# Closing norm of an expert-choice encoder layer: where six tiles meet the norm's weight, and in which order the last rows go

## What is computed

```python
def expert_choice_sublayer(x, norm_g, w_router, w_gate, w_up, w_down):
    tokens = rms_norm(x, norm_g).reshape(n_tok, d)
    affinity = softmax(tokens @ w_router)
    gate, idx = lax.top_k(affinity.T, cap)      # cap = 128 of 1024 tokens, 32 of 256
    xe = tokens[idx]
    hid = silu(xe @ w_gate) * (xe @ w_up)
    ye = (hid @ w_down) * gate[..., None]
    out = zeros.at[idx.reshape(-1)].add(ye.reshape(-1, d))
    return x + out
y = rms_norm(x, final_g)   # y * rsqrt(mean(y*y) + eps) * final_g
```

## Time and profile before

| | us |
|---|---|
| median of 3 runs | 1298.23 (1298.19 to 1299.98) |
| the profiled execution | 1298.81 |
| its span, first to last instruction | 1297.1 |
| last TensorE product of the last expert ends | 1279.85 |
| last VectorE instruction ends | 1292.17 |
| last indirect DMA issued | 1293.37 |

### The profile page before, as it was taken

The page is one execution under the profiler, slowest core; times in us unless marked ns, Lnnn a source line. Parts: engine busy times, 40 slices in busy tenths (PEclk is TensorE's granted clock), DMA queues, the critical chain, the costliest instruction groups (busy, mean ns, idle before and its releaser), DMA issues.

```text
span 1297.1 us, 25116 instructions
## 1 busy us (share of the span) xinstructions
PE 1255.2 (97%) x9762; PEld 1032.7 (80%) x9814; DVE 905.8 (70%) x1298; ACT 742.0 (57%) x1079; POOL 323.1 (25%) x316
## 2 busy tenths in 40 slices
PE   8999999999999999779999999999999999999994
PEld 7868986666687888578888888898889888988892
DVE  6462122541586655978879888988898889888887
ACT  7645322222345544456677667766676667667764
POOL 2512221010133231141132313131313231223040
PEclk8999999999999999979999999999999999999998
DMA  8231544360278773288999999999999999999996
GB/s 274 66 122 50 163 146 137 108 180 25 75 248 248 226 213 116 90 302 290 329 300 315 327 332 294 321 333 319 299 315 340 313 306 318 332 310 309 295 351 271
DMA packets 242033, 314.76 MB, mean 243 GB/s; under 512 B 16097, under 2 KB 206049, under 8 KB 241969
## 3 DMA queue, kind: packets, MB, share of 16 engines
q1 hardware_dynamic: 226576, 268.54, 62.3%
q0 software_dynamic: 15392, 45.36, 12.0%
HBM read 274.41 MB, written 39.44 MB: 242 GB/s over the span
## 4 chain that ended last, share of the span: by engine, by line
PE 92%; DMA 2%; ACT 2%; DVE 2%; issue 1%; SPq 0%; POOL 0%; ACTq 0%; DVEq 0%; POOLq 0%
PE psum L2253 23%; PE psum L2114 15%; PE psum L2260 11%; PE psum L2081 9%; PE psum L1965 9%; PE psum L2276 9%; PE psum L2294 4%; PE psum L2285 4%; PE psum L2246 1%; PE psum L2027 1%; DMA eraw<-in_w_up_dram 1%; PE psum L2032 1%; ACT yt L1248 1%; PE psum L1987 1%; PE psum L1945 1%
## 5 line engine op out<-in xcount | busy, mean ns | idle before, releaser
L1812 DVE TENSOR_TENSOR elo<-eraw,ehi 128x2048 bf16<-128x2048 f32 x192 | 433.5, 2285 | 1.0 <-POOLq L822 1.0
L1218 ACT ACTIVATE ehi<-eraw 128x2048 fp32r<-128x2048 f32 x192 | 362.2, 1902 | 25.7 <-PE psum L2294 18.6
L2253 PE MATMUL psum<-xc,ehi 128*128 128x320 f32 x2048 | 332.3, 314 | 1.9 <-DVE xc L1817 1.9
L2253 PEld LDWEIGHTS psum<-xc,ehi 128*128 128x128 f32 x2048 | 304.2, 189 | 3.5 <-DVE xc L1817 2.3
L2260 PE MATMUL psum<-xb,elo 128*128 128x160 bf16 x2048 | 163.9, 233 | 0.0
L1825 DVE TENSOR_REDUCE gu<-psum 128x320 f32<-128x640 f32 x128 | 105.3, 823 | 82.0 <-PE psum L2260 81.8
L2260 PEld LDWEIGHTS psum<-xb,elo 128*128 128x128 bf16 x2048 | 138.5, 98 | 13.0
L2114 PE MATMUL psum<-hn_nar,wnar 128*128 128x512 bf16 (+1 forms) x748 | 141.2, 343 | 1.2
L2276 PE MATMUL psum<-ehi,hc 128*128 128x512 f32 x512 | 132.7, 406 | 0.0
L2114 PEld LDWEIGHTS psum<-hn_nar,wnar 128*128 128x128 bf16 x768 | 73.1, 98 | 63.0 <-issue 4.5
L2276 PEld LDWEIGHTS psum<-ehi,hc 128*128 128x128 f32 x512 | 95.2, 188 | 22.1
(11 more groups left out here) (290 smaller groups left out, 1664.2 us busy)
## 6 DMA issues: line engine op xcount, KB each, us to landing
eraw<-in_w_gate_dram SPq DMA_DIRECT2D x64, 1024.0 KB, 6.6
eraw<-in_w_up_dram SPq DMA_DIRECT2D x64, 1024.0 KB, 9.6
eraw<-in_w_down_dram SPq DMA_DIRECT2D x64, 1024.0 KB, 13.6
wraw<-in_w_in_dram SPq DMA_DIRECT2D x12, 1024.0 KB, 7.3
negm<-negm_d SPq DMA_DIRECT2D x10, 512.0 KB, 7.4
acc_d<-x POOLq DMA_DIRECT2D x10, 512.0 KB, 5.4
tok_d<-tk POOLq DMA_DIRECT2D x10, 512.0 KB, 2.9
v<-v_d SPq DMA_DIRECT2D x18, 256.0 KB, 4.3
```

What stands on the lines that cost most here:

```text
L1218: act.activation(f["ehi"][:, j % RING, :], f["eraw"][:, raw_slot(s, j), :], ACT.Copy).then_inc(S["ehi"], 1)
L1812: dve.tensor_tensor(f["elo"][:, j % RING, :], f["eraw"][:, raw_slot(s, j), :], f["ehi"][:, j % RING, :].bitcast(F32), ALU.subtract).then_i ...
L2253: pe.matmul(o[:, 0:2 * NC], hi[:, k, c], x[:, k, :, :].rearrange("p a t -> p (a t)"), start=(k == 0), stop=False, skip_group_check=True)
```

## The change

The weight's part of six scalings goes to GpSimd: for k = 4 to 9 it multiplies the tile by the norm's weight into a new tile `pre`, which lies over the first three `ehi` buffers. The first of these waits for the last gate and up product (`gu_ps`), the fifth for the last expert's first down step (`dn_ps`), each pair for its tiles to have landed. VectorE scales four of the products (k = 4, 5, 8, 9) by the root alone with a `tensor_scalar`, and ScalarE two (k = 6, 7) with an ACTIVATE Copy. The roots are made in three batches (4, 4, 2) instead of two (4, 6). The last expert's rows are taken before the roots of k = 8 and 9. ScalarE's squares of k = 4 to 9 leave their unused output in PSUM instead of `yt`. The last two scatters, and the scalings ahead of them, change places: samples first, prompt second.

```diff
@@ -316,7 +316,9 @@
         FINAL = [0, 1, 8, 9, 2, 3, 4, 5, 6, 7]
-        FINAL_BATCHES = [(0, 4), (4, NT)]
+        FINAL_BATCHES = [(0, 4), (4, 8), (8, NT)]
+        BY_ACT = (6, 7)
+        pre = overlay(size([("eraw", [P, RAW, PIECE], F32)]), ("pre", [P, 6, D], F32))["pre"]
 
@@ -637,7 +640,10 @@
             for k, n in enumerate(FINAL):
-                sp.wait_ge(S["f_y"], k + 1)
+                if k in BY_ACT:
+                    sp.wait_ge(S["f_y_act"], k - BY_ACT[0] + 1)
+                else:
+                    sp.wait_ge(S["f_y"], k + 1 if k < BY_ACT[0] else k - 1)
                 sp.dma_start(y_chunk[n], final_tile(n)).then_inc(S["f_out_p" if n < NTP else "f_out"], 16)
@@ -861,17 +867,25 @@
             i.then_inc(S["f_same"], 1)
+            pool.wait_ge(S["gf_in"], 16 * 5)
+            for k in range(4, NT):
+                pool.wait_ge(f_in[k // 2], 32)
+                if k == 4:
+                    pool.wait_ge(S["gu_ps"], 8 * NE)
+                if k == 8:
+                    pool.wait_ge(S["dn_ps"], 4 * (NE - 1) + 1)
+                pool.tensor_tensor(pre[:, k - 4, :], final_tile(FINAL[k]), gf, ALU.mult).then_inc(S["f_pre"], 1)
             y_quarters = y_prompt[0].rearrange("t (j n) -> (t j) n", j=4)
+            pool.wait_ge(S["f_out"], 16 * NS)
+            pool.wait_ge(S["f_done"], 1)
+            settle()
+            pool.indirect_dma_start(y_sample[0], bass.IndirectOffsetOnAxis(ap=last_idx[:, 0:1], axis=0),
+                                    f["yt"][:, :], None).then_inc(S["f_set"], 16)
             pool.wait_ge(S["f_out_p"], 16 * NTP)
-            pool.wait_ge(S["f_done"], 1)
+            pool.wait_ge(S["f_done"], 2)
             settle()
...
                                     f["yp"][:, :], None).then_inc(S["f_set"], 16)
-            pool.wait_ge(S["f_out"], 16 * NS)
-            pool.wait_ge(S["f_done"], 2)
-            settle()
-            pool.indirect_dma_start(y_sample[0], bass.IndirectOffsetOnAxis(ap=last_idx[:, 0:1], axis=0),
-                                    f["yt"][:, :], None).then_inc(S["f_set"], 16)
             pool.wait_ge(S["f_set"], 32)
@@ -1245,7 +1259,8 @@
                         act.wait_ge(S["f_sum"], k)
-                    act.activation(f["yt"][:, :], final_tile(FINAL[k]), ACT.Square, scale=D ** -0.5,
+                    junk = f["yt"][:, :] if k < 4 else psum[:, 2:4, :].rearrange("p a n -> p (a n)")
+                    act.activation(junk, final_tile(FINAL[k]), ACT.Square, scale=D ** -0.5,
                                    accum_out=fs[:, 0, k:k + 1]).then_inc(S["f_sum"], 1)
@@ -1298,10 +1313,15 @@
             act.activation(fs[:, 3, 0:1], eps, ACT.Sqrt)
-            final_sums(*FINAL_BATCHES[1])
-            k0, k1 = FINAL_BATCHES[1]
-            act.wait_ge(S["f_sum"], k1)
-            act.activation(fs[:, 1, k0:k1], fs[:, 0, k0:k1], ACT.Sqrt, bias=eps).then_inc(S["f_root"], 1)
+            for k0, k1 in FINAL_BATCHES[1:]:
+                final_sums(k0, k1)
+                act.wait_ge(S["f_sum"], k1)
+                act.activation(fs[:, 1, k0:k1], fs[:, 0, k0:k1], ACT.Sqrt, bias=eps).then_inc(S["f_root"], 1)
+            act.wait_ge(S["f_polish"], 1)
+            for k in BY_ACT:
+                act.wait_ge(S["f_pre"], k - 3)
+                act.activation(final_tile(FINAL[k]), pre[:, k - 4, :], ACT.Copy, scale=fs[:, 1, k:k + 1]
+                               ).then_inc(S["f_y_act"], 1)
             act.wait_ge(S["f_row"], 1)
@@ -1879,15 +1899,28 @@
 
-            (_, first), (_, _) = FINAL_BATCHES
+            (_, first), (_, second), (_, _) = FINAL_BATCHES
+
+            def final_roots(k0, k1, batch):
+
+                dve.wait_ge(S["f_sum"], k1)
+                ch(dve.tensor_scalar(fs[:, 3, k0:k1], fs[:, 0, k0:k1], EPS, None, ALU.add))
+                dve.wait_ge(S["f_root"], batch)
+                polish(fs[:, 1, k0:k1], fs[:, 3, k0:k1], fs[:, 2, k0:k1])
+
+            def scale_weighted(k):
+
+                dve.wait_ge(S["f_pre"], k - 3)
+                dve.tensor_scalar(final_tile(FINAL[k]), pre[:, k - 4, :], fs[:, 1, k:k + 1], None, ALU.mult
+                                  ).then_inc(S["f_y"], 1)
+
             dve.wait_ge(S["f_sum"], first)
...
             scale_final(0, first)
-            dve.wait_ge(S["f_sum"], NT)
-            ch(dve.tensor_scalar(fs[:, 3, first:NT], fs[:, 0, first:NT], EPS, None, ALU.add))
-            dve.wait_ge(S["f_root"], 1)
-            polish(fs[:, 1, first:NT], fs[:, 3, first:NT], fs[:, 2, first:NT])
-            scale_final(first, NT - 2)
+            final_roots(first, second, 1)
+            dve.sem_inc(S["f_polish"], 1)
+            for k in range(first, BY_ACT[0]):
+                scale_weighted(k)
             dve.wait_ge(S["dn_ps"], 4 * NE)
@@ -1897,15 +1930,17 @@
                                          ALU.mult, ALU.add).then_inc(S["f_row"], 1)
-            scale_final(NT - 2, NT)
+            final_roots(second, NT, 2)
+            for k in range(second, NT):
+                scale_weighted(k)
             dve.wait_ge(S["f_sq"], 2)
             dve.tensor_scalar(fl[:, 2, 0:1], fl[:, 0, 0:1], EPS, None, ALU.add)
-            dve.wait_ge(S["f_root"], 3)
+            dve.wait_ge(S["f_root"], 4)
             ch(dve.tensor_scalar(fl[:, 2, 1:2], psum[:, 7, 0:1], EPS, None, ALU.add))
             polish(fl[:, 1, :], fl[:, 2, :], fl[:, 4, :])
+            dve.scalar_tensor_tensor(f["yt"][:, :], f["yt"][:, :], fl[:, 1, 0:1], gf, ALU.mult, ALU.mult
+                                     ).then_inc(S["f_done"], 1)
             dve.scalar_tensor_tensor(f["yp"][:, :], f["yp"][:, :], fl[:, 1, 1:2], gfq, ALU.mult, ALU.mult
-                                     ).then_inc(S["f_done"], 1)
-            dve.scalar_tensor_tensor(f["yt"][:, :], f["yt"][:, :], fl[:, 1, 0:1], gf, ALU.mult, ALU.mult
                                      ).then_inc(S["f_done"], 1)```

GpSimd, from its last gather to its last scatter, before (names in brackets are semaphores that the instruction waits for; `colS` holds the norm's weight):

```order
L850 DMA xg<-acc_d,idx 128x1024 [waits s_idx_cp,s_exT_ps]
L852 DMA xgp<-acc_d,idx 128x256
L855 MEMSET spare 128x1
L856 MEMSET spare 128x128
L859 AFFINE_SELECT spare<-spare 128x128 [waits s_pool_ch] x4
L868 DMA out_y_prompt_dram<-yp,idx 1024x256 [waits s_f_out_p,s_f_done]
L873 DMA out_y_sample_dram<-yt,last_idx 1024x1024 [waits s_f_out,s_f_done]
```

More of the change, by code:

```diff
@@ L344, in hybrid_conv_mlstm_moe @@
             "gu_ps gu_add sg_done hid_done hc_hi hc_lo hb_bf dn_ps y_done scat settled "
-            "conv_done cvl_done aff_out g2b_in tk_scaled gf_in f_in0 f_in1 f_in2 f_in3 f_in4 f_sum f_root f_y f_out f_out_p f_gath f_same f_row f_sq f_quart f_done f_set").split()}
+            "conv_done cvl_done aff_out g2b_in tk_scaled gf_in f_in0 f_in1 f_in2 f_in3 f_in4 f_sum f_root f_y f_out f_out_p f_gath f_same f_row f_sq f_quart f_done f_set "
+            "f_pre f_polish f_y_act").split()}
         x_in = (S["x_in0"], S["x_in1"], S["x_in2"], S["x_in3"], S["x_in4"])
```

## The result

The changed kernel takes 1307.23 us (median of 4, 1306.30 to 1308.16) against 1298.21 (median of 4): 1.0069 times as long, 95% interval 1.0056 to 1.0082. It is 9.0 us slower; 1304.6 was forecast, in a range of 1300.5 to 1308.5. The profiled execution's span is 1305.9 us against 1297.1.

The account below looks back on a forecast made before the run. VectorE sets the pace in the last 17.2 us; GpSimd's multiplications make its first full scaling 11.2 us late, with a gain of about 5 us behind; span 1303.5 against 1297.1, so 1304.6 us by the median, range 1300.5 to 1308.5.

Parts of the forecast that it names:

- VectorE stands for whole multiplications, the two taking turns: From 1268.5, each GpSimd multiplication holds VectorE, which enters at each change; first full scaling 11.2 us late; chance 0.62.
- The rival with VectorE kept out: VectorE stands through all six GpSimd multiplications; `hid` ends at 1282.9; span 1305.4, time 1306.5; chance 0.14.
- the one without hindrance: GpSimd's reads of the tiles leave VectorE alone or VectorE wins most turns; span 1293.4, time 1294.5; chance 0.16.
- the one in which only long instructions are held: Short 128x4 first-root instructions slip through, full scalings alternate with multiplications; time 1302.7; chance included in the 0.62 for turns.
- One or two short instructions a pause: First roots' twelve 0.2 us instructions: one or two run between multiplications, so six remain at 1283, 1.2 us.
- The chain behind it: VectorE alone from about 1284.2: four scalings, roots, light scalings, rows, roots, `yt`, ending at 1298.0.
- Covers: `hid` 1.5 us late doesn't delay TensorE's prompt products; ScalarE's sums of k = 4 to 9, moved 1.5 us, are covered.
- lands 2.7 us on: Last plain store (k = 9, 1295.7) lands 2.7 us later, at 1298.4 to 1298.6.
- The 0.93 for the start: GpSimd's first scatter starts 0.5 to 0.9 us behind the last plain store's landing, at 1299.1; 0.93 was measured before.
- The standing of the earlier trace: VectorE `STT` at 353.43 stood through six GpSimd instructions and five changes, taking 4.81 us instead of 1.21.

Follow-up runs that it names:

- the first two runs: Changed kernel without GpSimd's six multiplications: 1295.58 us; kernel before with those six multiplications added and their products unused: 1308.21 us.
- the run with the multiplications alone: Kernel before with GpSimd's six multiplications added at the same place, products unused: 1308.21 us, 1.0076 times before.
- the run with two multiplications and PSUM: Changed kernel, but GpSimd multiplies only k = 6 and 7, after the first roots; VectorE's full scalings read the weight from PSUM: 1296.16 us.

## Why the prediction was right, and where its size was short

- *VectorE stands for whole multiplications, the two taking turns.* As forecast: `hid` ended 1271.19 (forecast 1271.3), the low part of `hc` 1273.74 (1273.7), GpSimd worked from 1268.47 to 1282.95 (1268.5 to 1283). VectorE came in at each of the five changes. The rival with VectorE kept out is excluded (`hid` would have ended at 1282.9, TensorE at 1286.8), the one without hindrance too (the first two runs), and so is the one in which only long instructions are held. The time alone would not have settled it: 1307.23 lies 0.2 us above the forecast's own range of 1302 to 1307, and the 1306.5 of the kept-out rival is nearer to it than 1304.6. It is the trace that tells the two apart.
- *One or two short instructions a pause.* It was one each time: four were done by 1283, eight were left, where the sum had six and six. That is 0.4 us: the first full scaling came at 1284.60 instead of 1284.2. I hadn't been sure that the two `tensor_scalar`s of four elements would be held; they were, for 2.3 us each.
- *The chain behind it.* Four scalings, roots, light scalings, rows, roots, `yt`: end at 1298.18, forecast 1298.0. The light scalings took 0.71 a piece in a row, ScalarE's 1.1.
- *Covers.* TensorE's end didn't move; ScalarE's sums came 1.4 us later (1273.37 against 1271.96) and were done at 1280.85, long before VectorE wanted them.
- *The term that was mis-sized* is the landing of the last plain store: "lands 2.7 us on". It took 4.6 (1300.6 instead of 1298.4 to 1298.6), and GpSimd's 0.95 behind it came in full, where the sum had 0.5. The landing's 1.9 and the start's 0.45 are nearly all of the 2.4 us between the forecast span, 1303.5, and 1305.9. The 0.93 for the start stood in the sum as its upper bound, from the row of before. The sum for the case without hindrance did have the six stores paced at 1.28 us; in the sum of the forecast I took the unhurried 2.7 although the light scalings bunch the stores there just as much: six issues between 1291.30 and 1296.0, where before they were spread over 1281.88 to 1289.6. The same pacing from 1291.30 on, 1.4 + 6 x 1.28, gives 1300.4, 0.2 us from what was measured.
- The case without hindrance, 1293.4 of span, was measured as 1294.1 by the run without multiplications; its last plain store, too, took 4.7 us to land.

What stays open is how GpSimd hands over. In the changed kernel and in the run with the multiplications alone VectorE came in at every one of the ten changes between multiplications. The standing of the earlier trace rows, which the prediction took for a single case, is not one: the same instruction stands at the same place in all ten traces. In nine of them it lasts 4.80 to 4.82 us and ends behind all six GpSimd instructions (four multiplications of 0.7 us and two selects). In the run with two multiplications and PSUM it lasts 4.34 and came in ahead of the second select, which then waited (2.31 us for the two selects instead of 1.22). The changed kernel first, then that run:

```profile
L1561 DVE SCALAR_TENSOR_TENSOR wol<-woraw,woh x1: 4816/4816/4816, 352.8 to 352.8; 128x1024 fp32r<-128x1024 f32 x1
355.32 1.22 POOL L713 TENSOR_SCALAR_AFFINE_SELECT E<-E 128x512 f32<-128x512 f32 x2
...
L1560 DVE SCALAR_TENSOR_TENSOR wol<-woraw,woh x1: 4340/4340/4340, 353.0 to 353.0; 128x1024 fp32r<-128x1024 f32 x1
355.52 2.31 POOL L714 TENSOR_SCALAR_AFFINE_SELECT E<-E 128x512 f32<-128x512 f32 x2
```

So one turn per GpSimd instruction held for the 2.4 us multiplications here, and not for this row of short ones. The two places differ in the length of GpSimd's instructions and in the waits between them, among other things, and no run tells which of it matters.

## What to carry to other kernels

Before work is given to GpSimd beside VectorE, look at where VectorE's operands lie at that time, not at how much GpSimd is idle: in these runs a GpSimd multiplication that reads SBUF held every VectorE instruction with two SBUF tensors and every `tensor_scalar` in SBUF that met it, down to 4 elements a row, until it was through (up to 2.35 us). A chain of small dependent instructions is then the worst neighbour. With one operand of VectorE's instruction in PSUM, the two ran side by side at full speed. And when the scalings get lighter, the stores behind them bunch: cost the last landing by the queue (here one 512 KB store every 1.2 to 1.3 us), not by the median of stores that were spread out. Last, compare two traces from a common instruction close to the change: the work ahead of it moved a span by up to 1.5 us.

## What the runs showed of the hardware that I had not expected

- `tensor_scalar` on 128x4 elements waits for GpSimd memsets (0.73 to 0.90 us for 0.17), while two-tensor instructions beside them don't wait at all (`hid` 0.49 us, full scalings 1.24 a piece).
- Each hold costs nearly a whole multiplication even for four elements: 2.26 to 2.35 us against 0.16.
- A full scaling with the weight in PSUM is as fast as from SBUF (1.276 against 1.280 us), and copying the 128x1024 weight there took 1.22 us, nearly all of it in a gap of 1.20 us that VectorE had anyway (`hid` then starts 0.09 us behind the end of the Silu instead of 0.03).
